# A decoder layer with 32 experts: gate and up weights laid in 8 KB runs, and the output norm's passes kept in PSUM

## What is computed

```python
h = layer_norm(ALPHA * x + hybrid_token_mixer(x, ...), ln1_g, ln1_b)
...
def hierarchical_moe(x, ...):
    ...                      # softmax over 4 groups, the best group, its best 2 of 8 experts, their weights
    hg = jnp.einsum("td,edf->tef", t, exp_w_gate)      # 32 x 1024 x 256
    hu = jnp.einsum("td,edf->tef", t, exp_w_up)        # 32 x 1024 x 256
    hid = jax.nn.silu(hg) * hu * combine[:, :, None]
    out = jnp.einsum("tef,efd->td", hid, exp_w_down)   # 32 x 256 x 1024
...
h = layer_norm(ALPHA * h + ffn, ln2_g, ln2_b)
```

## Time and profile before

| what | us |
|---|---|
| median of 3 runs | 437.44 |
| lowest, highest | 436.12, 437.76 |
| the profiled execution, its own device time | 435.74 |
| span of the profiled execution (first to last instruction) | 433.9 |

### The profile page before, as it was taken

One profiled execution on the slowest core, in us unless ns is written; L12 is line 12 of the kernel. 1 busy time (PEld: TensorE's weight loads), 2 busy tenths in 40 slices (PEclk: granted clock), 3 DMA queues, 4 the chain that ended last, 5 costly groups with the idle time before them and its releaser, 6 DMA issues.

```text
span 433.9 us, 6632 instructions
## 1 busy us (share of the span) xinstructions
PE 409.5 (94%) x2578; PEld 276.5 (64%) x2578; DVE 187.3 (43%) x368; ACT 114.6 (26%) x185; POOL 83.5 (19%) x113
## 2 busy tenths in 40 slices
PE   7999999999999999999999999999999878888793
PEld 6888877888888888865555555556555544453331
DVE  3569522699955388854222122212221212111077
ACT  4442387953132003211111111111111101001411
POOL 2220000000000001122332333233323311210124
PEclk9999999999999999999999999999999989898997
DMA  8865532033379999999999999999999999999584
GB/s 276 268 192 181 190 98 77 22 97 98 97 251 415 415 412 421 415 375 408 406 406 409 410 405 408 409 408 406 411 412 410 409 413 411 412 412 417 217 332 193
DMA packets 45569, 139.11 MB, mean 321 GB/s; under 512 B 5107, under 2 KB 17427, under 8 KB 41446
## 3 DMA queue, kind: packets, MB, share of 16 engines
q1 hardware_dynamic: 39376, 126.89, 75.3%
q0 software_dynamic: 6144, 11.84, 7.5%
q10 hardware_dynamic: 22, 0.02, 0.0%
HBM read 134.41 MB, written 12.58 MB: 339 GB/s over the span
## 4 chain that ended last, share of the span: by engine, by line
PE 80%; DMA 11%; DVE 5%; SPq 2%; issue 1%; ACT 0%; DVEq 0%; ACTq 0%
PE bank L1088 21%; PE bank L902 12%; PE bank L903 12%; PE bank L904 12%; PE bank L1117 10%; DMA wgu<-in_exp_w_up 5%; DMA wgu_first<-in_exp_w_up 5%; PE bank L1078 3%; PE bank L1108 2%; SPq L500 2%; PE bank L1179 2%; DVE stats L1572 1%; PE bank L885 1%; PE bank L1055 1%; PE bank L962 1%; DMA raw<-in_w_in 1%
## 5 line engine op out<-in xcount | busy, mean ns | idle before, releaser
L1088 PE MATMUL bank<-wgu,xTg 128*64 128x256 f32 x736 | 87.9, 394 | 7.5 <-DMA wgu<-in_exp_w_up 6.7
L1088 PEld LDWEIGHTS bank<-wgu,xTg 128*64 128x64 f32 x736 | 52.9, 141 | 35.2 <-DMA wgu<-in_exp_w_up 7.6
L902 PE MATMUL bank<-xT_hi,w_hi 128*128 128x512 f32 x160 | 63.0, 394 | 0.9 <-DVE xT_lo L1228 0.9
L903 PE MATMUL bank<-xT_lo,w_hi 128*128 128x512 f32 x160 | 62.4, 390 | 0.0
L904 PE MATMUL bank<-xT_hi,w_lo 128*128 128x512 f32 x160 | 62.4, 390 | 0.0
L1528 DVE TENSOR_TENSOR hid<-gated,bank 64x256 f32<-64x256 f32 x32 | 13.5, 423 | 112.1 <-ACT gated L834 112.0
L674 POOL DMA_INDIRECT y_pairs<-ys,y_rows x32 | 32.5, 1016 | 140.7 <-PE bank L1078 105.1
L834 ACT ACTIVATE gated<-bank 64x256 f32<-64x256 f32 x32 | 12.1, 377 | 136.8 <-PE bank L1088 136.8
L1117 PE MATMUL bank<-wdn,hidT 128*64 128x512 f32 x192 | 45.4, 593 | 0.0
L1205 DVE TENSOR_TENSOR w_lo<-raw,w_hi 128x2048 fp32r<-128x2048 f32 x12 | 27.5, 2288 | 26.6 <-ACT w_hi L748 26.6
L669 POOL DMA_INDIRECT xg<-h_rows,x_rows x31 | 31.4, 1014 | 24.7 <-issue 8.3
(11 more groups left out here) (255 smaller groups left out, 499.0 us busy)
## 6 DMA issues: line engine op xcount, KB each, us to landing
wgu<-in_exp_w_gate SPq DMA_DIRECT2D x24, 1024.0 KB, 19.9
wgu<-in_exp_w_up SPq DMA_DIRECT2D x24, 1024.0 KB, 21.8
wdn<-in_exp_w_down SPq DMA_DIRECT2D x24, 1024.0 KB, 21.5
raw<-in_w_in SPq DMA_DIRECT2D x9, 1024.0 KB, 5.3
raw<-in_w_out SPq DMA_DIRECT2D x4, 1024.0 KB, 5.0
wdn_extra<-in_exp_w_down SPq DMA_DIRECT2D x4, 1024.0 KB, 22.2
wgu_spare<-in_exp_w_gate SPq DMA_DIRECT2D x4, 1024.0 KB, 18.9
wgu_spare<-in_exp_w_up SPq DMA_DIRECT2D x4, 1024.0 KB, 21.2
```

The costliest lines, as they stand in the source:

```text
L902: pe.matmul(dst, a_hi, b_hi, start=start, stop=False)
L903: pe.matmul(dst, a_hi, b_lo, start=False, stop=False)
L1088: mm = pe.matmul(psum[2 + b][BLOCK * which:BLOCK * which + BLOCK, 0:F], xTg[b][:, j, h * BLOCK:(h + 1) * BLOCK], wgu[s][:, which, k, :], s ...
```

## The change

Four edits, of which the first needs the second.

1. `gu_of` and `gu_place`: partition p gets rows 8p to 8p + 7 of gate and of up, one run of 8 KB for each matrix in place of two of 4 KB. Chunk k of `wgu` now holds row 8p + k.
2. The columns of the residual are ordered for it. The first norm's second pass writes half h of `xres` as the columns c with (c // 4) % 2 = h, which it reads in groups of four out of every eight from a new tile `scaled` and from `ln_b` (`dealt`). `turn_h1` takes columns with a step of four; the router weights are loaded with the same order of rows; the final product reads h1 back in order (`in_order`). Everything between (h1_rows, gathers, `turn_x`, `gate_up`) is the same code.
3. The output norm: `z_of` is PSUM for tile 0 too; the first pass writes to PSUM in place of `pair_y`, the second reads PSUM and writes `pair_y`. `shift` is computed by `tensor_scalar` in place of `scalar_tensor_tensor`.
4. The nine diagonals are made in ACT's item 31, ahead of its gate, in place of after the loop.

```diff
+        scaled = sb("scaled", [P, D])
...
         def z_of(t, h):
-            return pair_y[t][1][:, h * H:(h + 1) * H] if t < DVE_ADDED else psum[2 * t + h][:, :]
+            return psum[2 * t + h][:, :]
...
+        def dealt(rows, a):
+
+            return rows[:, :].rearrange("p (m a j) -> p a m j", a=2, j=4)[:, a, :, :]
+
+        def in_order(rows):
+
+            return rows.rearrange("p (a m j) -> p m a j", a=2, j=4)
...
-            return w.rearrange("a (h p j) f -> p (a h) (j f)", h=2, p=P)
+            return w.rearrange("a (p k) f -> p (a k f)", p=P)
...
-            return wgu[s][:, which, :, :].rearrange("p (h j) f -> p h (j f)", h=2)
+            return wgu[s][:, which, :, :].rearrange("p k f -> p (k f)")
...
-            pool.dma_start(wr[:, :, N_GROUPS:NR], router_expert_w.rearrange("(k p) n -> p k n", p=P)).then_inc(router_in, 16)
+            pool.dma_start(wr[:, :, N_GROUPS:NR], router_expert_w.rearrange("(p k) n -> p k n", p=P)).then_inc(router_in, 16)
...
+            def make_diagonals():
+
+                act.wait_ge(gu_summed, 4 + 3 * RING)
+                act.activation(diag[:, 0, :], ident[:, :], ACT.Copy, scale=ALPHA).then_inc(diag_ready, 1)
+                act.wait_ge(weights_ready, 1)
+                for t in range(TT):
+                    for k in range(TOP_K):
+                        act.activation(diag[:, 1 + TOP_K * t + k, :], ident[:, :], ACT.Copy, scale=weight[:, k, t:t + 1]).then_inc(diag_ready, 1)
+
             def act_item(q, r):
+                if static(r) and q == N_EXP - 1:
+
+                    make_diagonals()
...
-                        mm = pe.transpose(psum[4 + 2 * (t % 2) + n][:, k * P:(k + 1) * P], xres[:, t, (4 * n + k) * P:(4 * n + k + 1) * P], ident[:, :])
+                        cols = xres[:, t, n * H:(n + 1) * H].rearrange("p (m j) -> p j m", j=4)[:, k, :]
+                        mm = pe.transpose(psum[4 + 2 * (t % 2) + n][:, k * P:(k + 1) * P], cols, ident[:, :])
...
-                    pe.matmul(psum[2 * t + h][:, :], diag[:, 0, :], h1[:, t, h * H:(h + 1) * H], start=True, stop=False)
+                    pe.matmul(psum[2 * t + h][:, :], diag[:, 0, :], in_order(h1[:, t, :])[:, h * H // 8:(h + 1) * H // 8], start=True, stop=False)
...
-                link(v.scalar_tensor_tensor(out=xres[:, t, :], in0=xres[:, t, :], scalar=moments[:, t, 0:1], in1=ln_g[:, :], op0=ALU.subtract, op1=ALU.mult))
+                link(v.scalar_tensor_tensor(out=scaled[:, :], in0=xres[:, t, :], scalar=moments[:, t, 0:1], in1=ln_g[:, :], op0=ALU.subtract, op1=ALU.mult))
...
-                    v.scalar_tensor_tensor(out=part, in0=part, scalar=rstd[:, t:t + 1], in1=ln_b[:, h * H:(h + 1) * H],
+                    v.scalar_tensor_tensor(out=part.rearrange("p (m j) -> p m j", j=4), in0=dealt(scaled, h), scalar=rstd[:, t:t + 1], in1=dealt(ln_b, h),
...
-                        step(v.scalar_tensor_tensor(out=z_of(t, h), in0=z_of(t, h), scalar=weight[:, 1, t:t + 1], in1=psum[2 * t + h][:, :],
+                        step(v.scalar_tensor_tensor(out=z_of(t, h), in0=pair_y[t][1][:, h * H:(h + 1) * H], scalar=weight[:, 1, t:t + 1], in1=z_of(t, h),
...
-                    step(v.scalar_tensor_tensor(out=pair_y[t][1][:, cols], in0=z_of(t, h), scalar=moments[:, t, 0:1],
-                                                in1=ln2g[:, cols], op0=ALU.subtract, op1=ALU.mult))
+                    step(v.scalar_tensor_tensor(out=z_of(t, h), in0=z_of(t, h), scalar=moments[:, t, 0:1],
+                                                in1=ln2g[:, h * H:(h + 1) * H], op0=ALU.subtract, op1=ALU.mult))
...
-                    v.scalar_tensor_tensor(out=shift[:, t:t + 1], in0=moments[:, t, 0:1], scalar=-1.0, in1=rstd[:, t:t + 1],
-                                           op0=ALU.mult, op1=ALU.mult).then_inc(moments2_ready, 1)
+                    v.tensor_scalar(shift[:, t:t + 1], moments[:, t, 0:1], rstd[:, t:t + 1], -1.0, ALU.mult, ALU.mult).then_inc(moments2_ready, 1)
...
-                    z = pair_y[t][1][:, h * H:(h + 1) * H]
-                    v.scalar_tensor_tensor(out=z, in0=z, scalar=rstd[:, t:t + 1], in1=ln2b[:, h * H:(h + 1) * H],
+                    cols = slice(h * H, (h + 1) * H)
+                    v.scalar_tensor_tensor(out=pair_y[t][1][:, cols], in0=z_of(t, h), scalar=rstd[:, t:t + 1], in1=ln2b[:, cols],
```

More of the change, by code:

```diff
@@ L639, in _ @@
             pool.wait_ge(ln1_in, 32)
[L640 removed]
+            pool.dma_start(wr[:, :, 0:N_GROUPS], router_group_w.rearrange("(p k) n -> p k n", p=P)).then_inc(router_in, 16)
             pool.wait_ge(router_in, 16)
[L642 removed]
+            pool.dma_start(wr[:, :, N_GROUPS:NR], router_expert_w.rearrange("(p k) n -> p k n", p=P)).then_inc(router_in, 16)
             pool.dma_start(rbias[:, 0:N_GROUPS], row(router_group_b).to_broadcast([P, N_GROUPS])).then_inc(router_in, 16)
@@ L861, in _ @@
             overflow(act, act_over)
-            act.activation(diag[:, 0, :], ident[:, :], ACT.Copy, scale=ALPHA).then_inc(diag_ready, 1)
-            act.wait_ge(weights_ready, 1)
-            for t in range(TT):
-                for k in range(TOP_K):
-                    act.activation(diag[:, 1 + TOP_K * t + k, :], ident[:, :], ACT.Copy, scale=weight[:, k, t:t + 1]).then_inc(diag_ready, 1)
             for t in range(TT):
```

2 lines of the change are left out of this document (removed).

## The result

| kernel | median us | runs, lowest to highest | ratio to before, 95% interval |
|---|---|---|---|
| before (same chip) | 436.25 | 6, 435.17 to 437.76 | |
| changed | 433.49 | 6, 432.06 to 434.47 | 0.9938 (0.9912 to 0.9964) |

The change makes the kernel faster by 0.6%: 2.7 us, with an interval from 1.6 to 3.8. The forecast was 433.5 us, a gain of 3.9 against the median of 437.44 that it started from. The profiled execution of the changed kernel has 433.34 us, its span 431.5; outside the span lie 1.84 us, as before.

The account below looks back on a forecast made before the run. Bound by the weight stream from expert 7 to the last gate and up: -3.6 (stream) + 0.1 (routing chain) - 0.4 (end) = -3.9 us, from 437.44 to 433.5 us; range 430.3 to 437.0.

Parts of the forecast that it names:

- the one of 5.4 us: Stretch with 4 KB packets alone at 410 GB/s; priced the expert weight stream's gain from 8 KB runs at 3.6 us.
- the one of 2.9 us: Stretch with 4 KB packets alone at 420 GB/s; stream gains only 0.6 us, as a rival 436.5 us, chance 0.13.
- 1.69 us at the last product: Rival: last gate and up at full clock saves 1.69 us, the end gains 1.9, total 432.0 us; chance 0.20.

Follow-up runs that it names:

- e7: The changed kernel again, without an edit, for a second profile: 433.47 us, ratio 0.9942 to the kernel before.
- e1: The kernel before with only the 8 KB runs of gate and up and the column order they need: 433.25 us, ratio 0.9907.

## What to carry over

Where a stream of weights without a pause is the bound, count packets as well as bytes: with some 10 ns a packet and DMA engine between 2 and 8 KB, a layout that turns two runs into one is worth it, and its price can be estimated from stretches of a single packet size. Short ones disagree: here the one of 5.4 us was right and the one of 2.9 us was not, so a run at a second packet size is worth more than either. Then find where the stream starts and what can delay that start, since this is paid in full. And before taking a gain at the end for granted, ask which transfer an earlier one will meet: here 1.69 us at the last product became 0.7 at the end.

## What the runs showed of the hardware

- A price per packet: with gate and up in 2, 4 and 8 KB runs the same stretch of the stream, 50 such transfers, took 217.44, 208.75 and 205.04 us. From 8 to 2 KB that is 10.3 ns, from 8 to 4 KB 9.3 ns, for each packet more on an engine.
- The TensorE clock isn't the same in each execution of one kernel. The first six products took 0.63 us each (read as 1.2 GHz) in two profiles of the changed kernel and 0.40 (2.4 GHz) in the third, after the same work and waits of 0.79, 1.08 and 1.11 us; in the two the transposes ahead of them had all taken 421 ns, in the third the last ones 273. The last gate and up of the changed kernel took 3.67 us (granted clock 1.00 in its first 3.2 us) or 5.36 (0.52), after a wait of 2.03 us both times. Both move a single execution by 0.7 to 1.4 us.
- The profile's granted clock can miss a slow start: it reads 1.00 from 8 to 11 us in the changed kernel and in e7, and 0.50 in e1, while the products of that stretch take 0.63 us in all three.
- The last indirect scatter takes 3.1 to 3.3 us until its successor is issued when it comes late enough to have the DMA engines nearly to itself, and 4.25 to 4.27 beside the norm's weights and the last of h1; without those weights it took 3.44.
- The two passes of the output norm on DVE take 737 to 751 ns for 128 x 512: the source, SBUF or PSUM, makes no difference beyond a few ns (743 and 740), and writing PSUM some 10 ns more (751 against 740). A one-column instruction on DVE with two SBUF operands took up to 0.58 us while POOL worked on two SBUF operands, 0.21 as `tensor_scalar`.
